# A hybrid streaming encoder layer on one core: expert tiles of two 64-slot halves, two weight rings, and the first stage's loads in another order

## The reference, cut to what matters

```python
mod = silu(c) @ w_ada + b_ada                     # shift1, scale1, gate1, shift2, scale2, gate2
h = rms_norm(x) * (1 + scale1) + shift1
proj = h @ w_in                                   # S5 input, q, k, v, indexer parts, two gates
x = x + gate1 * (merged(S5 branch, sparse attention branch) @ w_out)
h2 = rms_norm(x) * (1 + scale2) + shift2
# router: best of 4 groups, in it the best 2 of 4 experts; combine[n, e] their weights
hid = silu(h2 @ w_gate[e]) * (h2 @ w_up[e])       # 16 experts, 1024 -> 256
x = x + gate2 * sum_e(combine[:, e] * hid) @ w_down[e]      # 256 -> 1024
```

## Time and profile before

| | us |
|---|---|
| median of 3 runs | 1543.55 (1543.49 to 1547.27) |
| the profiled execution | 1545.17, its span 1543.4 |
| TensorE busy | 1372.2 (89% of the span) |
| gate-up, down, transposes of x in the expert stage, TensorE busy | 185.2, 93.6, 30.9 |
| DMA moved | 193.04 MB, 125 GB/s on the mean |

### The profile page before, as it was taken

How to read it: one execution, slowest core, us unless ns; L and a number is a source line. 1 busy time by engine, 2 the same in 40 slices (tenths; PEclk the granted TensorE clock), 3 DMA queues, 4 the chain that set the end, 5 groups by cost and what they waited for, 6 DMA issues and landing times. The chain is left out here.

```text
span 1543.4 us, 20736 instructions
## 1 busy us (share of the span) xinstructions
PE 1372.2 (89%) x7461; PEld 797.9 (52%) x7462; DVE 817.8 (53%) x1722; ACT 443.3 (29%) x963; POOL 253.4 (16%) x454
## 2 busy tenths in 40 slices
PE   3899996988989899999959998989992599999994
PEld 2555553666734466666626665644441444544542
DVE  0422222886577788989955555334235444444433
ACT  3321111232355466765135555001111000000000
POOL 0000002003010011111100000000000245555553
PEclk8899998998989999999989999999996599999998
DMA  8500015764031422321050000542326479886752
GB/s 325 182 3 5 32 36 139 226 194 53 11 86 48 145 82 86 127 71 57 30 199 1 2 1 2 203 140 96 109 86 225 146 245 313 279 310 213 245 178 74
DMA packets 141563, 193.04 MB, mean 125 GB/s; under 512 B 33125, under 2 KB 108837, under 8 KB 141253
## 3 DMA queue, kind: packets, MB, share of 16 engines
q1 hardware_dynamic: 120092, 151.43, 29.8%
q0 software_dynamic: 17904, 37.23, 7.5%
q10 hardware_dynamic: 3482, 3.23, 0.8%
HBM read 159.75 MB, written 53.42 MB: 138 GB/s over the span
## 5 line engine op out<-in xcount | busy, mean ns | idle before, releaser
L2270 PE MATMUL ps<-ex_wgu,ex_xT 128*128 x416 | 185.2, 599 | 0.3 <-issue 0.3
L1391 DVE TENSOR_SCALAR_CACHE_REDUCE tk_eq<-sc,tk_cand 128x512 bf16<-128x512 f32 (+4 forms) x155 | 146.8, 1007 | 0.0
L1789 PE MATMUL ps<-hT,mergedT 128*128 128x512 f32 (+1 forms) x288 | 120.1, 600 | 4.9 <-DMA op_wr<-in_w_route_expert 4.9
L2270 PEld LDWEIGHTS ps<-ex_wgu,ex_xT 128*128 128x128 f32 x416 | 77.8, 192 | 89.1 <-issue 89.0
L1325 PE MATMUL ps<-zT,gt_w 128*128 128x352 f32 (+1 forms) x384 | 120.9, 468 | 0.0
L1325 PE MATMUL ps<-hT,gt_w 128*128 128x352 f32 (+1 forms) x336 | 105.8, 468 | 0.0
L1325 PEld LDWEIGHTS ps<-zT,gt_w 128*128 128x128 f32 x384 | 73.0, 190 | 44.0
L2290 PE MATMUL ps<-ex_wd,ex_hidT 128*128 x208 | 93.6, 593 | 2.0 <-DVE ex_hidT L2343 2.0
L1354 ACT ACTIVATE mask<-sc,tk_cand 128x384 bf16<-128x384 f32 (+1 forms) x62 | 82.2, 1329 | 15.0 <-DVE tk_cand L1407 15.0
L1789 PEld LDWEIGHTS ps<-hT,mergedT 128*128 128x128 f32 (+1 forms) x288 | 50.9, 186 | 68.3 <-issue 62.7
L2336 DVE SCALAR_TENSOR_TENSOR ex_hid<-ex_silu,ex_weight,ps 128x256 f32<-128x256 f32 x26 | 12.5, 480 | 135.6 <-ACT ex_silu L2314 135.6
(11 more groups left out here) (484 smaller groups left out, 2282.4 us busy)
## 6 DMA issues: line engine op xcount, KB each, us to landing
ex_wgu<-in_w_gate SPq DMA_DIRECT2D x16, 1024.0 KB, 7.2
ex_wgu<-in_w_up SPq DMA_DIRECT2D x16, 1024.0 KB, 10.1
ex_wd<-in_w_down SPq DMA_DIRECT2D x16, 1024.0 KB, 5.6
sp_ada_w<-in_w_ada SPq DMA_DIRECT2D x9, 1024.0 KB
merge_left_dram<-qiT SPq DMA_DIRECT2D x8, 544.0 KB, 6.4
mg_gb<-gate_b_dram SPq DMA_DIRECT2D x8, 544.0 KB, 3.9
mergedT<-merge_left_dram SPq DMA_DIRECT2D x8, 544.0 KB, 4.9
u<-in_w_ada SPq DMA_DIRECT2D x2, 2048.0 KB, 13.2
```

What stands on the lines that cost most here:

```text
L1391: return v.tensor_scalar(junk[j], m.sc[0:r, c:c + w], scalar, 0.0, op, ALU.add, accum_out=cnt[0:r, j:j + 1])
L1789: i = nc.tensor.matmul(m.ps[rows, 2 * (t % 2) + n, :], m.mergedT[:, k, t * P:t * P + r], m.wout[:, k, n * 512:(n + 1) * 512], start=k == 0 ...
L2270: j = nc.tensor.matmul(m.ps[:, 2 + b, :], xT[:, b, k, :], wgu[:, bass.ds(at, 1), k, :].rearrange("p o n -> p (o n)"), start=k == 0, stop=k ...
```

## The change

- An expert tile holds 64 slots of an expert of side 0 (groups 0 and 3) and 64 slots of an expert of side 1 (groups 1 and 2). Slots 0 to 63 are the stationary operand's columns 0 to 63 and give PSUM partitions 0 to 63; the others give the upper half. Each half multiplies with its own expert's weights.
- Gate-up is split into two halves h of the hidden width: for each h and each of 8 k, two products (one per side) of 64 stationary and 256 moving columns. Down: for each f and c two products of 64 by 512.
- On TensorE one tile is finished before the next begins: gate-up h=0 and h=1, hidden transpose 0, transposes of tile n+1, hidden transpose 1, down f=0, down f=1. `xg`, `xT`, `hidT` and `gate` have one buffer instead of two.
- TensorE and ScalarE run eight loops, one for each expert of side 1, with one tile in a turn; in these the buffer of side 1 is known, and that of side 0 comes from `tile_place`. The loop bounds are read from `expert_done` between two loops.
- Each side has a ring of two buffers (four in place of three). SP loads side 0, ScalarE side 1. Before the experts, SP loads four experts' weights.
- The routing counts in 64s, per side, and its one-hot tables lie in `hT`; a table has 42 tiles (`MAXT`) in place of 34.
- First stage: the x tiles are loaded one, one, two and five at a time, each group behind one of the weight loads, and normalised in these groups; the fourth slice's modulation rows come before the second x tile, and the projections start after two x tiles.

```diff
-RING = 3
-MAXT = (2 * NT + NE * P) // P
+RING, HALF = 2, P // 2
+SIDES = ((0, 3), (1, 2))
+MAXT = 2 * NT // HALF + NE // 2
...
+        normed = ((0,), (1,), (2, 3), (4, 5, 6, 7, 8))
                 for i in range(NB):
                     load_w(i)
-                    for t in range(3 * i, 3 * i + 3):
-                        load_x(t)
+                load_x(0)
                 sp.wait_ge(ps, 1)
                 load_w(NB)
-                for sem, lo, hi in ((wlq, 512, 1024), (wlr, 1024, OFF_GA), (wlu, 0, 512)):
+                load_x(1)
+                for sem, lo, hi, tiles in ((wlq, 512, 1024, (2, 3)), (wlr, 1024, OFF_GA, (4, 5, 6, 7, 8)), (wlu, 0, 512, ())):
                     sp.dma_start(pw[:, :, lo:hi], wp[:, :, lo:hi]).then_inc(sem, 16)
+                    for t in tiles:
+                        load_x(t)
...
                 x_transposes(0)
+                mod_rows(NB)
+                columns(NB).then_inc(colt, 1)
                 pe.wait_ge(gqe, 1)
                 x_transposes(1)
-                mod_rows(NB)
-                columns(NB).then_inc(colt, 1)
+                queries(0)
                 x_transposes(2)
-                queries(0)
+                rest(0)
...
+                def norm_x(k):
+                    c = slice(normed[k][0], normed[k][-1] + 1)
+                    dve.wait_ge(ssq, c.stop)
+                    v.tensor_scalar(st1[:, 1, c], st1[:, 0, c], 1.0 / D, EPS, ALU.mult, ALU.add).then_inc(msx, 1)
+                    dve.wait_ge(sr, k + 1)
+                    step(v.reciprocal(st1[:, 3, c], st1[:, 2, c]))
+                    for t in normed[k]:
+                        r = rows_of(t)
+                        v.tensor_scalar(x[0:r, t, :], x[0:r, t, :], st1[0:r, 3, t:t + 1], None, ALU.mult).then_inc(xnr, 1)
...
+        def expert_by_expert(engine, tile, ahead=None, behind=None):
+            for j in range(EACH):
+                start = end_of(engine, 1, j - 1) if j else 0
+                end = end_of(engine, 1, j)
+                if ahead:
+                    ahead(j)
+                with engine.Fori(start, end) as n:
+                    tile(n, j)
+                if behind:
+                    behind(j, end)
...
+                def gate_up(n, j, at, h):
+                    w = (wgu[:, bass.ds(at, 1), :, :].rearrange("p o k (a n) -> p (o k) a n", a=2),
+                         wgu[:, RING + j % RING, :, :].rearrange("p k (a n) -> p k a n", a=2))
+                    for k in range(KD):
+                        for side, mine in enumerate(place_of):
+                            i = nc.tensor.matmul(m.ps[mine, 2 + h, 0:FD], xT[:, k, mine], w[side][:, k, :, P * h:P * (h + 1)],
+                                                 start=k == 0, stop=k == KD - 1)
+                    i.then_inc(gp, 1)
...
+                def down(n, j, at, f):
+                    pe.wait_ge((hta, htd)[f], n + 1)
+                    w = (wd[:, bass.ds(at, 1), f, :].rearrange("p o n -> p (o n)"), wd[:, RING + j % RING, f, :])
+                    for c in range(2):
+                        for side, mine in enumerate(place_of):
+                            i = nc.tensor.matmul(m.ps[mine, 4 + c, :], hidT[:, f, mine], w[side][:, 512 * c:512 * (c + 1)],
+                                                 start=f == 0, stop=f == 1)
...
+                def tile(n, j):
+                    at = pe.value_load(m.tile_place[0:1, bass.ds(n, 1)], min_val=0, max_val=RING - 1)
+                    ready = pe.value_load(m.tile_ready[0:1, bass.ds(n, 1)], min_val=1, max_val=EACH)
                     pe.wait_ge(here, ready)
                     pe.wait_ge(xed, n + 1)
                     pe.wait_ge(xea, n + 1)
...
+                    gate_up(n, j, at, 0)
+                    gate_up(n, j, at, 1)
+                    hidden_transpose(n, 0)
+                    transposes(n + 1)
+                    hidden_transpose(n, 1)
+                    pe.wait_ge(yed, n + 1)
+                    down(n, j, at, 0)
+                    down(n, j, at, 1)
...
+                def next_weights(j, end):
+                    if j + RING < EACH:
+                        load_gate_up(act, m, A, 1, j + RING)
+                        act.wait_ge(dn, end)
+                        load_down(act, m, A, 1, j + RING)
```

More of the change, by code:

```diff
@@ L353, in _ @@
                 act.wait_ge(dv, 1)
[L354 to L362, removed]
+                root(0)
                 act.wait_ge(ps, n)
@@ L436, in _ @@
                     j.then_inc(rowc, 1)
[L437 to L443, removed]
+                    if i == NB - 1:
+                        norm_x(0)
+                norm_x(1)
                 dve.wait_ge(colt, 1)
@@ new lines, in _ @@
+                tiles, done, start, first = (ex[:, j, :] for j in range(4))
+                step(ts(exi[:, 0, :], base[:, TILES, :], HALF - 1.0, None, ALU.add))
+                step(ts(exi[:, 1, :], exi[:, 0, :], 6, None, ALU.logical_shift_right))
+                of_side = lambda a, side: a.rearrange("p (g j) -> p j g", g=NG)[:, :, SIDES[side][0]:SIDES[side][1] + 1:SIDES[side][1] - SIDES[side][0]]
+                for side in range(2):
+                    mine = slice(NE // 2 * side, NE // 2 * (side + 1))
+                    step(ts(tiles[:, mine].rearrange("p (j g) -> p j g", g=2), of_side(exi[:, 1, :], side), 1.0, None, ALU.max))
+                    step(v.tensor_tensor_scan(done[:, mine], m.ones[:, 0:NE // 2], tiles[:, mine], 0.0, ALU.mult, ALU.add))
@@ new lines, in _ @@
+                step(tt(start, done, tiles, ALU.subtract))
+                for side in range(2):
+                    mine = slice(NE // 2 * side, NE // 2 * (side + 1))
+                    step(ts(of_side(first, side), start[:, mine].rearrange("p (j g) -> p j g", g=2), float(P), float(HALF * side),
+                            ALU.mult, ALU.add))
+                choice = lambda c: s16[:, c].rearrange("p t g j -> p t (g j)")
+                for c in range(2):
+                    step(tt(choice(2), choice(c), tot[:, :, :], ALU.mult))
+                    step(v.tensor_reduce(s1[:, 10 + c, :], choice(2), AX.X, ALU.add))
+                    step(tt(choice(c), choice(c), bc(first, 1, TILES), ALU.mult))
+                    step(v.tensor_reduce(s1[:, 7 + c, :], choice(c), AX.X, ALU.add))
@@ L2140, in wait_alone, with run @@
             nc.gpsimd.tensor_tensor(idle[:, place:place + 1], idle[:, 0:1], idle[:, 0:1], ALU.add)
-        def run(engine, body, before=None, after=None):
+        def run(engine, body, before, after):
             loops = engine.value_load(m.loops[0:1, 0:1], min_val=LOOPS[0], max_val=LOOPS[1])
-            if before:
-                before()
+            before()
             body(0)
@@ L2283, in down @@
-                def down(i, b):
-                    n = 2 * i + b
-                    at = place(n)
-                    pe.wait_ge(htc, n + 1)
-                    wait(pe, yed, n)
-                    for c in range(2):
-                        for f in range(2):
-                            j = nc.tensor.matmul(m.ps[:, 4 + c, :], hidT[:, b, f, :],
-                                                 wd[:, bass.ds(at, 1), f, 512 * c:512 * (c + 1)].rearrange("p o n -> p (o n)"),
-                                                 start=f == 0, stop=f == 1)
-                    j.then_inc(dn, 1)
@@ L2295, in body @@
-                def body(i):
-                    for b in range(2):
-                        gate_up(i, b)
-                        previous(down, i, b)
-                        hidden_transposes(i, b)
-                        transposes(i + 1, b)
-                run(pe, body, lambda: (transposes(0, 0), transposes(0, 1)), lambda last: down(last, 1))
+                    gate_up(n, j, at, 0)
+                    gate_up(n, j, at, 1)
+                    hidden_transpose(n, 0)
+                    transposes(n + 1)
@@ L2310, in silu, with xts @@
-                def silu(i, b):
-                    n = 2 * i + b
-                    act.wait_ge(gp, n + 1)
-                    wait(act, hr, n - 1)
-                    nc.scalar.activation(sl[:, b, :], m.ps[:, 2 + b, 0:FD], ACT.Silu).then_inc(slr, 1)
-                def body(i):
-                    for b in range(2):
-                        silu(i, b)
-                        xts(i + 1, b)
-                run(act, body, lambda: (xts(0, 0), xts(0, 1)))
+                def xts(n):
+                    act.wait_ge(tp, 2 * n + 2)
+                    nc.scalar.copy(xT[:, 4:8, :].rearrange("p k n -> p (k n)"), m.ps[:, 1, :]).then_inc(xea, 1)
@@ L2323, in _ @@
+                xts(0)
+                expert_by_expert(act, tile, behind=next_weights)
             @block.vector
```

306 lines of the change are left out of this document (155 added, 151 removed).

## The result

The changed kernel takes 1508.55 us (1506.33 to 1509.96, 4 runs) against 1545.41 (1543.49 to 1548.51, 4 runs) for the kernel before: a ratio of 0.9752, 95% interval 0.9731 to 0.9774. The forecast was 1518, its own range 1500 to 1535.

| stretch | predicted | measured |
|---|---|---|
| start to the first queries | -9.7 | 52.71 to 42.66: -10.05 |
| from there to the start of routing | 0 | -10.05 becomes -6.8 (1176.1 to 1169.3): +3.2 |
| routing, to the first expert transposes | +2.9 | 42.6 to 45.7: +3.1 |
| those to the first gate-up | -1.0 | 4.20 to 2.88: -1.3 |
| first gate-up to the last down product | -18.7 | 302.9 to 274.2: -28.7 |

The account below looks back on a forecast made before the run. TensorE's own time was taken to bound the expert stage, and loads the start. Expert stage -18.7, routing +2.9, the expert stage's earlier start -1.0, first stage -9.7 sum to -26.5: 1518 us, own range 1500 to 1535.

Parts of the forecast that it names:

- Overlap of the halves: In an expert tile's products, both column halves run side by side: gate-up passes 107 ns apart, 215 without overlap.
- Tiles: Expert stage: 22 tiles replace 26, each 11.9 us (bounds 11.4 and 13.0), together 261.8 us.
- Expert changes: Between two experts of side 1, seven times, two loop-bound reads in the open cost 1.5 us: 10.5 in all, bounds 0 and 17.5.
- Start and end of the stage: Expert stage: its start and end add 5 us to the tiles, of 6.9 in the kernel before.
- Weights late at tile 4: Expert stage: side 0's third expert's weights come late at tile 4 alone, 7 us, bounds 0 and 14.
- ScalarE's issue of side 1's loads ... no cost: Expert stage: ScalarE's load issue stands before the next silu, nearly 4 us into the next tile, and costs nothing.
- Routing +2.9: Routing: added VectorE steps and wider tables make it 2.9 us longer, bounds 2 and 4.
- the first stage -9.7: First stage: the queries start at 42.0 us, not 52.71, for a gain of 9.7 us, bounds -13.5 and -4.
- no overlap: Rival, expert tile products: the halves don't overlap, the stage takes 201 us more, the whole 1738 us; chance 0.03.
- the turn of the loop: Rival, TensorE's sequencer at each tile's branch: code fetches cost 2.5 us a tile, 55 in all, 1573 us; chance 0.07.
- Weights late: Rival, expert stage: of 12 reloads five or six more come 5 us late, 27 us, 1545 us; chance 0.09.
- Nothing shows: Rival, expert stage: reads are hidden and weights in time, the stage -45 us, the whole 1492 us; chance 0.17.

## Why the prediction held, and where its terms were off

The deciding step, the overlap of the halves, was right in its mechanism. That the sum came as near as 9 us is in part luck: four of its terms for the expert stage were too high by 18.8 us together (tiles 3.5, changes 6.5, start and end 1.8, weights 7), and one loss of 8.9 us that it did not have took half of that back. With the measured terms the stage is 258.3 + 4.0 + 3.2 + 8.9 = 274.4, against 274.2.

- **Overlap of the halves:** right. 108 ns a pass was forecast as 107, from the attention's products. What that row could not show is the condition, which the kernel meets by turning sides at every product. The Trainium skill (TensorE: Matmul & The Clock Gate, Part 3, "The mechanism") lets a weight load run beside products in flight only where the row groups differ. Here both halves use all rows, and in the 274.2 us of the stage TensorE was busy with products for 263.1 and with weight loads for 149.5, so most of the loads did run beside products, and the trace disagrees. The same section of the Trainium skill gives TensorE a window of 64 instructions in which a weight load may be pulled ahead; for the products of the other half the runs show far less, about four passes at a turn of sides.
- **Tiles:** 22 x 11.9 was forecast, 22 x 11.74 = 258.3 measured, 3.5 us less, and the gap of 0.3 us before each gate-up is not there. The sequencer was counted as free at 11.5 to 11.8 us of a tile; it is through its reads at about 11.0 (1295.1, in the tile that began at 1284.11), and 1.0 us of cover is left.
- **Expert changes:** mis-sized. 1.5 us in the open at seven places was forecast, 0.57 was measured: 4.0 instead of 10.5. The reads cost what was said, 2 x 0.73; the step took the cover to be used up by the tile's own two reads, and 1.0 of it was left, as the four extra reads showed.
- **Start and end of the stage:** 5 was forecast; the first gate-up's slower passes, 8.53 for 6.91, are the visible part, and with the seven gate-ups behind a gap (7.13 for 6.91) it comes to 3.2.
- **Weights late at tile 4:** 7 us forecast, and a wait of some 3 us, with 1.7 of slower gate-up behind it, would have come there, as the run with down weights on SP showed. In the changed kernel itself TensorE has no such wait, because another one covers it.
- **"ScalarE's issue of side 1's loads ... no cost":** this step failed. The position in the list was read rightly, nearly 4 us ahead of the next silu, but no length was put on the issue itself; it took 9.42 and 9.07 us where both sides reloaded at once, and 8.9 us were lost. Taking the loads off ScalarE gave 8.2 us in the stage. In the kernel before it cost nothing: SP issued all weights, and no computation stands behind SP's issues.
- **Routing +2.9, the start of the stage -1.0, the first stage -9.7:** measured +3.1, -1.3, -10.05. The rows of routing and the first transposes now are:

```profile
L1998 SPq DMA_DIRECT2D rt_bias<-in_b_route_group x1: 333/333/333, 1169.3 to 1169.3; - x1
```

```profile
1215.02 1.97 PE L2302 MATMUL ps<-ident,ex_x 128*128 128x128 f32 x8 [8.21 <-DMA ex_x<-h_dram,ex_idx]
```

- **Rivals:** *no overlap* and *the turn of the loop* fell with the chain of one tile, which has no gap. *Weights late* was there in one place of twelve. *Nothing shows* (1492) is near what is left when loads and reads are out of the way, 1497.6.

## What to carry to other kernels

A load's issue is an instruction of the engine that issues it, and its length follows the queue's state; 0.4 us is what an idle one took here. Put loads that may follow each other closely on an engine with no work behind them, or count how many of them stand in that queue unmoved, above all while another queue is being served. Register reads cost 0.7 us each here and are free only under cover, so ask at each place how far ahead the sequencer is, and when moving them look for a wait that is there anyway. Two column halves gave the full factor of two here when they took turns every one or two products.

## What the runs showed of the hardware

- Issuing a load of 1 MB took 0.37 us at the least. ScalarE's third load, 3.5 to 3.6 us behind its first, took 0.37 three times, where its queue had moved 0.6 MB meanwhile, and 3.72, 9.07 and 9.42 where it had moved 0.04, none and 0.14 MB while SP's moved 1.04, 0.98 and 0.87. The longest of all was 10.85, in the run with turns of four products. With gate and up alone on ScalarE no issue took over 0.8.
- Two column halves that share all 128 rows overlap fully in float32: 6.91 us for 64 passes of 256 columns and 3.58 for 16 of 512. Turning sides every four products: 8.16; every eight: 11.34.
- A value read by TensorE's sequencer costs 0.73 us with its register work; two more of them at an expert change make a gap of 0.57 us, four more in a plain tile one of 1.9.
- Executions of one program differ by some 6 us in when they reach routing, 1164.5 to 1170.4.
